# Block kernel, two-head recurrent part: the diagonal of the scores as products on VectorE, summed over the features by TensorE with a tile of ones

## The reference

```python
q = silu(hg_q) * HG_DK ** -0.5
log_f = log_sigmoid(hg_f)              # the lower bound is zero for the only layer
k = 1 - exp(log_f)                     # = sigmoid(-hg_f)
...
b = cumsum(log_f)                      # over the tokens of a chunk, per feature
decay = exp(where(s <= t, b[t] - b[s], -inf))
scores[t, s] = sum_over_features(q[t] * k[s] * decay[t, s])
o[t] = q[t] * exp(b[t]) @ state + scores[t, :] @ v
```

## Time and profile before

| | |
|---|---|
| median of 3 executions | 3282.65 us (3281.4 to 3282.71) |
| profiled execution, its own time | 3283.14 us |
| its span, first to last instruction | 3281.4 us |
| TensorE matmuls busy | 3260.9 us (99%) |
| TensorE weight loads busy (beside the matmuls) | 2811.7 us (86%) |
| VectorE busy | 2207.2 us (67%) |
| ScalarE busy | 1721.2 us (52%) |
| GpSimd busy | 314.2 us (10%) |
| chain that ended last | TensorE 97%, VectorE 2%, ScalarE 1% |

### The profile page before, as it was taken

The page is one execution under the profiler, slowest core; times in us unless marked ns, Lnnn a source line. Parts: engine busy times, 40 slices in busy tenths (PEclk is TensorE's granted clock), DMA queues, the critical chain, the costliest instruction groups (busy, mean ns, idle before and its releaser), DMA issues.

```text
span 3281.4 us, 54604 instructions
## 1 busy us (share of the span) xinstructions
PE 3260.9 (99%) x17950; PEld 2811.7 (86%) x17950; DVE 2207.2 (67%) x3262; ACT 1721.2 (52%) x2555; POOL 314.2 (10%) x378
## 2 busy tenths in 40 slices
PE   8999999999999999999999999999999999999999
PEld 7888888888888888888888888888888888888888
DVE  6666766677655867666666677887555557665666
ACT  5444444455555665444444456774444446555554
POOL 1000000011100301000000001220222221100000
PEclk9999999999999999999999999999999999999999
DMA  6566566555555655666666656556545555555555
GB/s 232 187 199 188 185 192 188 185 180 165 180 173 186 190 166 174 191 190 187 189 187 189 188 178 196 184 178 193 161 155 158 155 158 174 182 170 179 176 171 165
DMA packets 280057, 592.46 MB, mean 181 GB/s; under 512 B 19856, under 2 KB 171664, under 8 KB 279840
## 3 DMA queue, kind: packets, MB, share of 16 engines
q1 hardware_dynamic: 278816, 587.12, 57.5%
q10 hardware_dynamic: 1152, 4.19, 0.3%
HBM read 589.14 MB, written 2.10 MB: 180 GB/s over the span
## 4 chain that ended last, share of the span: by engine, by line
PE 97%; DVE 2%; ACT 1%; issue 0%; DMA 0%; POOL 0%; SPq 0%; ACTq 0%
PE bank L566 45%; PE bank L565 11%; PE bank L568 11%; PE bank L607 8%; PE bank L609 8%; PE bank L608 8%; PE bank L798 2%; PE bank L810 1%; DVE w_low L1564 1%; DVE normed L1609 0%; PE bank L692 0%; PE bank L762 0%; ACT w_high L1073 0%; PE bank L700 0%; PE bank L795 0%
## 5 line engine op out<-in xcount | busy, mean ns | idle before, releaser
L1564 DVE TENSOR_TENSOR w_low<-w_raw,w_high 128x1024 fp32r<-128x1024 f32 (+1 forms) x1120 | 1355.7, 1219 | 639.3 <-ACT w_high L1073 620.5
L1073 ACT ACTIVATE w_high<-w_raw 128x1024 fp32r<-128x1024 f32 (+1 forms) x1120 | 1167.1, 1045 | 753.8 <-PE bank L609 398.4
L566 PE MATMUL bank<-normed,w_high 128*128 128x512 f32 x3968 | 1264.4, 397 | 11.1 <-DVE w_low L1564 10.4
L566 PE MATMUL bank<-mixed,w_high 128*128 128x512 f32 x2432 | 769.8, 396 | 1.8 <-DVE increment L1596 1.7
L566 PEld LDWEIGHTS bank<-normed,w_high 128*128 128x128 f32 x3968 | 610.1, 189 | 12.7 <-issue 10.4
L565 PE MATMUL bank<-normed,w_low 128*128 128x256 f32 x1984 | 552.9, 279 | 0.0
L568 PE MATMUL bank<-normed,w_low 128*128 128x256 f32 x1984 | 550.9, 278 | 0.0
L607 PE MATMUL bank<-w_high,normed 128*128 128x512 f32 x1152 | 462.9, 402 | 1.1 <-DVE w_low L1564 1.1
L565 PEld LDWEIGHTS bank<-normed,w_low 128*128 128x128 f32 x1984 | 373.0, 188 | 90.7
L609 PE MATMUL bank<-w_high,normed 128*128 128x512 f32 x1152 | 449.7, 390 | 0.0
L608 PE MATMUL bank<-w_low,normed 128*128 128x512 f32 x1152 | 449.3, 390 | 0.0
(11 more groups left out here) (311 smaller groups left out, 2227.3 us busy)
## 6 DMA issues: line engine op xcount, KB each, us to landing
w_raw<-w_att SPq DMA_DIRECT2D x128, 512.0 KB, 3.5
w_raw<-w_up1a SPq DMA_DIRECT2D x64, 512.0 KB, 4.2
w_raw<-w_up1b SPq DMA_DIRECT2D x64, 512.0 KB, 4.0
w_raw<-w_up2a SPq DMA_DIRECT2D x64, 512.0 KB, 3.8
w_raw<-w_up2b SPq DMA_DIRECT2D x64, 512.0 KB, 3.8
w_raw<-w_rg SPq DMA_DIRECT2D x64, 512.0 KB, 4.1
w_raw<-w_hg SPq DMA_DIRECT2D x64, 512.0 KB, 3.6
w_raw<-w_hg SPq DMA_DIRECT2D x128, 256.0 KB, 2.8
```

Of the source, the lines that this page charges most:

```text
L566: last = nc.tensor.matmul(banks[b][:, :], hi, x, start=starts and k == 0, stop=stop)
L1073: A_(wh[slot][:, 0:width], raw[slot][:, 0:width], ACT.Copy).then_inc(wh_done, 1)
L1564: TT(wl[slot][:, 0:width], raw[slot][:, 0:width], wh[slot][:, 0:width].bitcast(F32), ALU.subtract).then_inc(wl_done, 1)
```

## The change

For the pairs of wide heads round 0 is computed in another way. VectorE multiplies q by k element by element (three operations of 128x512: the product rounded to the format of the split weights, the product in full, and the difference of the two), and writes the high and the low part into the two rows of `Y` that later take the output of the same pair. TensorE then multiplies a 128x128 tile of ones with the high row and with the low row, two products of 128x512 accumulated in one bank: every partition of the bank receives the sum over the features, so the masked copy picks the same diagonal as before. The copy stays as it was, and so do rounds 1 to 8. In the tables, the new VectorE step `product` stands at place 9 behind the store of the pair before, and round 0 moves from ahead of unit 10 into its middle, directly ahead of round 1. It waits for a new semaphore, `multiplied`, instead of `prepared`. One copy of 128x128 makes the rounded tile of ones at the start of the stage.

```diff
+        ones_r = sb("ones_rounded", [P, P], F32R)
...
-        dec = handoffs("decay", "prepared summed grown started masked round updated placed")
+        dec = handoffs("decay", "prepared multiplied summed grown started masked round updated placed")
...
-                8: [("prepare", 0)], 9: [("store", 1)], 10: [(0, 0)]}
-        IN_H = {0: [(7, 1)], 1: [(8, 1)]} | {j: [(j - 9, 0)] for j in range(10, 16)}
+                8: [("prepare", 0)], 9: [("store", 1), ("product", 0)]}
+        IN_H = {0: [(7, 1)], 1: [(8, 1)]} | {j: [(j - 9, 0)] for j in range(11, 16)} | {10: [(0, 0), (1, 0)]}
...
-                    if step == 0:
+                    if step == 0 and heads == 1:
                         pe.wait_ge(dec["prepared"], it + 1)
+                    if step == 0 and heads == 2:
+                        pe.wait_ge(dec["multiplied"], it - HEADS_G + 1)
...
+                    if heads == 2 and step == 0:
+                        rows = [Y[:, bass.ds((it - HEADS_G) * 2 + n, 1), :].rearrange("p a s -> p (a s)") for n in range(2)]
+                        nc.tensor.matmul(b_out[:, :], ones_r[:, :], rows[0], start=True, stop=False)
+                        nc.tensor.matmul(b_out[:, :], ones_r[:, :], rows[1], start=False, stop=True).then_inc(dec["round"], 1)
+                        return
...
-                        rhs = B if step == 0 and heads == 2 else C
+                        rhs = C
...
+                if step == "product":
+                    dve.wait_ge(dec["prepared"], it + 1)
+                    if not isinstance(it, int):
+                        dve.sem_inc(dve_passed, 1)
+                    high, low_ = Y[:, bass.ds(y0, 1), :], Y[:, bass.ds(y0 + 1, 1), :]
+                    high, low_ = (r.rearrange("p a (h s) -> p (a h) s", h=2) for r in (high, low_))
+                    TT(high, B[:, 0:2, :], B[:, 2:4, :], ALU.mult)
+                    own.did(TT(Dm[:, 2:4, :], B[:, 0:2, :], B[:, 2:4, :], ALU.mult))
+                    own.settle()
+                    TT(low_, Dm[:, 2:4, :], high.bitcast(F32), ALU.subtract).then_inc(dec["multiplied"], 1)
...
+                    nc.vector.tensor_copy(ones_r[:, :], ones[:, :])
```

More of the change, by code:

```diff
@@ L2393 @@
 PER = {"act_gla": 0, "act_rg": 4, "act_hg": 0, "act_att": 0,
-       "dve_gla": 0, "dve_rg": 9, "dve_hg": 0, "dve_att": 21}
+       "dve_gla": 0, "dve_rg": 9, "dve_hg": 1, "dve_att": 21}
 def tiled(m, tiles_k):
```

## The result

| | before | changed |
|---|---|---|
| median of 5 executions | 3282.65 us (3281.4 to 3282.75) | 3317.95 us (3316.26 to 3319.63) |
| ratio | | 1.0108, 95% interval 1.0096 to 1.0119 |
| span of the profiled execution | 3281.4 us | 3316.2 us |
| TensorE busy | 3260.9 us | 3271.7 us |
| VectorE busy | 2207.2 us | 2223.8 us |

The kernel is slower by 35.3 us, 4.4 for each of the eight pairs of heads. The forecast was 31.7 us slower, the range 3303 to 3323. VectorE's 16.6 us more are its 24 new operations and the one copy of the ones. TensorE's busy time grew although the change takes products from it; part of this is a lower clock, as will be seen.

The account below looks back on a forecast made before the run. TensorE was taken to bound the kernel, busy 3260.9 of 3281.4 us. Stops 23.2 + 3.1, less gain 3.4, plus clock 8.8 gave +31.7 us on 3282.65, so 3314.4 us; range 3303 to 3323.

Parts of the forecast that it names:

- The gain: TensorE, wide heads: two products with ones replace the old round 0, saving 0.43 us a pair, 3.4 us for eight.
- The stop: TensorE waits for VectorE's product at the first product with ones: 23.2 us for seven loop pairs, 3.1 net for the first.
- The clock: TensorE's clock falls at most of the eight stops after 3.1 us of idleness, 1.1 us each, 8.8 us.
- Some stops may escape: TensorE's clock: a reason for taking 1.1 us a fall, since not every one of the eight stops might bring it down.
- Round 1 behind the stop costs the same at both levels: TensorE's clock: a reason for 1.1 us; round steps are 0.11 already, and 128 columns at the lower level give 0.11.
- The upper bound: Price of one clock fall, at most 2.6 us, from TensorE's slow stretch of 5.5 us at the start of the kernel.
- What else moves: VectorE's 16.8 us more and its later low halves and copies, and GpSimd's operations, were expected to stay hidden.
- Hidden by 1 us or more: VectorE's copies of rounds 0 and 1 end near 2371.3; round 2 needs only the first, at about 2372.8.
- The price that the prediction gave for work without cover: Low half of unit 13 on VectorE ends 2.1 us later; without the cover of three units it would cost 2.1.
- The clock didn't hold: Rival that the clock holds: the stop stays, the clock term goes, +22.9 us, 3305.6 us; chance 20%.
- Ready in time: Rival: VectorE's product ends before 2365.4, so only the bare gain of 3.4 us remains, 3279.2 us; chance 3%.
- the step would have to come first on VectorE: Condition for the product being ready: only 2.2 us from `prepared` for 2.1 us of operations, while instruction order puts it third.

Follow-up runs that it names:

- e5_pe_alone: Kernel before with only TensorE's part: round 0 is two 128x512 products of other tiles, at its old place and wait, diagonal wrong; 3278.49 us, ratio 0.9988.
- e1_filled: Changed kernel with 13 unneeded 128x512 products on TensorE ahead of each wait for the product; 3305.2 us, ratio 1.007.
- e4_high: Changed kernel with one VectorE operation instead of three, both products with ones reading the high row, diagonal wrong; 3294.29 us, ratio 1.0036.
- e6_dve_alone: Kernel before with three more VectorE operations at place 9, their result read by nobody, round 0 unchanged; 3296.79 us, ratio 1.0043.
- e8_early_later: Changed kernel with VectorE's product at place 8, ahead of the store, and all rounds one unit later; 3281.54 us, ratio 0.9998.
- e2_early: Changed kernel with VectorE's three operations one place earlier, at place 8, ahead of the low half of unit 12 and the store; 3293.13 us, ratio 1.0035.
- e3_swap: Changed kernel with VectorE's product ahead of the store at place 9; 3309.24 us, ratio 1.008.
- e7_later: Changed kernel with all rounds one unit later and VectorE's product where the change put it; 3284.72 us, ratio 1.0008.
- e9_swap_later: Changed kernel with the rounds one unit later and VectorE's product ahead of the store at place 9; 3282.22 us, ratio 1.0.

## Why the prediction was right, and where it wasn't

**The gain.** 3.4 us reckoned, 3.6 measured (e5_pe_alone).

**The stop.** 26.3 us less the gain, 22.9, reckoned; 22.8 measured (e1_filled). In the second pair the first product with ones ends at 2372.04 in the chain of waits; the product before it ended at 2368.40, so 2368.63 was possible: 3.4 us lost, 3.3 reckoned. Every part held: the order of VectorE's instructions, 2.12 us for the three operations, the hand-over through an address instruction (2371.38 to 2371.54).

**The clock.** This is the term that was mis-sized: 1.1 us a stop, 1.6 measured, and that is nearly all of the 3.6 us by which the forecast was low (0.5 x 8 = 4.0). That the clock would fall at most stops was right. The size was a choice between two bounds, and two of the reasons for taking it low did not hold. "Some stops may escape": none did. "Round 1 behind the stop costs the same at both levels": it doesn't. The prediction compared a quarter of a 128x512 product at the lower level, 0.11 us, with the steps of a round at the higher one, 0.11; but a step of a round slows down as well, and a round that lies wholly in the slow stretch takes 1.71 us instead of 0.89 (e4_high, first pair). So it doesn't matter whether the slow stretch falls on round 1 or on the products behind it: 3.4 us at half the clock lose 3.4 x (1 - 0.23/0.43) = 1.6 us in either case, and the traces show 1.6 for each fall, whether it came 0.06 or 1.4 us after the restart. The upper bound, 2.6 from the start of the kernel, held as a bound.

**What else moves.** "Hidden by 1 us or more" for VectorE's copies was right for the change, but only because TensorE stood still meanwhile. Without the stop the three operations cost 14.7 us, 1.8 a pair (e6_dve_alone). The price that the prediction gave for work without cover, 2.1 a pair, is near this; what it missed is where the cover is thin. It looked for it at the low halves (three units). The thin place is the copy of round 0, which stands behind the low half of unit 13 and in front of round 2's bank. The stop hid this second delay.

**The rivals.** The clock didn't hold. "Ready in time", with the decision at the end of the product, was priced at 3279.2: e8_early_later, where it is in time, came to 3281.5, because the later rounds and, by subtraction, GpSimd's collision take back 0.45 us a pair, for which the rival had no term. That the step would have to come first on VectorE was not enough (e2_early): there it runs into GpSimd.

## What to carry to other kernels

When a step moves to another engine, ask first when that engine will have done what stands ahead of it, and when the receiver arrives; the busy shares (58% of VectorE in this stage) say nothing about a single place. Price a stop of TensorE twice, once for the time and once for the clock if the rest is long, and look at what the engines behind it would have done without the stop, since one delay can hide another. A saving of 0.4 us a pair is only worth a move if the tables around it have that much room: none of the five ways to shorten or remove the stop with the whole product (e2_early, e3_swap, e7_later, e8_early_later, e9_swap_later) kept the gain.

## What the runs showed of the hardware that was not expected

- The clock falls late. In the changed kernel it was granted in full during the whole rest of 3.15 us and for 0.7 to 1.4 us of the work behind it, and then the lower level lasted 3.4 us, while TensorE was busy all the time.
- Between 2.1 and 2.5 us the length of the rest alone doesn't tell whether the clock falls: 2.06 brought it down and 2.15 didn't, 2.5 did at 5 of 7 stops.
- A fall costs 1.6 us whatever lies in the slow stretch: a round of 128x128 products in full precision takes 1.71 us there instead of 0.89.
- Useless products pay: 13 of them ahead of each wait made the changed kernel 12.8 us faster.
- GpSimd and VectorE stop each other for whole instructions: 1.66 us for 0.68 on VectorE (e2_early), 1.70 for 0.87 on GpSimd (e9_swap_later); they ended only 0.54 and 0.72 us after the other's instruction.
